# Pairs of output tiles of the gated feed-forward by seven products of quarters, in a two-layer decoder step

## The reference

```
D_MODEL = 1024;  D_FF = 2816
def rms_norm(x, g):
    xf = x.astype(jnp.float32)
    y = xf * lax.rsqrt(jnp.mean(xf * xf, axis=-1, keepdims=True) + NORM_EPS)
    return (y * g.astype(jnp.float32)).astype(x.dtype)
def swiglu(x, w_gu, w_down):
    g, u = jnp.split(x @ w_gu, 2, axis=-1)
    return (jax.nn.silu(g) * u) @ w_down
...
# in each of the two layers, behind the attention:
h = h + swiglu(rms_norm(h, g_ffn), w_gu, w_down)
```

## Time and profile before

| | |
|---|---|
| median of 3 runs | 1571.15 us (1570.95 to 1577.21) |
| the profiled execution | 1575.01 us, its span 1572.5 us |
| PE busy | 1441.2 us, 92% of the span |
| DVE / ACT / POOL busy | 427.7 / 338.4 / 197.9 us |
| moved between HBM and the chip's memory | 235.75 MB |
| granted clock of PE, mean | 0.933 of full speed |

### The profile page before, as it was taken

One profiled execution on the slowest core, in us unless ns is written; L12 is line 12 of the kernel. 1 busy time (PEld: TensorE's weight loads), 2 busy tenths in 40 slices (PEclk: granted clock), 3 DMA queues, 4 the chain that ended last, 5 costly groups with the idle time before them and its releaser, 6 DMA issues.

```text
span 1572.5 us, 22763 instructions
## 1 busy us (share of the span) xinstructions
PE 1441.2 (92%) x8680; PEld 1054.4 (67%) x8680; DVE 427.7 (27%) x1061; ACT 338.4 (22%) x885; POOL 197.9 (13%) x315
## 2 busy tenths in 40 slices
PE   7996889689899999999999999978788799999996
PEld 4454667457787788777777764675545477777775
DVE  2606454431222120111110017627534212111000
ACT  2115443321222120110000001336633201000000
POOL 0111292000000000211110111150022211111000
PEclk9995999789999999999999999857799799999998
DMA  7349687675355530334333451440056644342340
GB/s 276 108 134 359 219 312 243 232 257 174 114 170 168 195 112 0 101 114 158 109 127 111 144 181 59 148 126 1 1 161 203 214 160 161 107 160 99 110 139 30
DMA packets 145620, 235.75 MB, mean 150 GB/s; under 512 B 9554, under 2 KB 101970, under 8 KB 145106
## 3 DMA queue, kind: packets, MB, share of 16 engines
q1 hardware_dynamic: 140386, 212.39, 40.3%
q0 software_dynamic: 5136, 22.05, 4.1%
HBM read 229.09 MB, written 13.64 MB: 154 GB/s over the span
## 4 chain that ended last, share of the span: by engine, by line
PE 84%; DVE 5%; ACT 4%; DMA 3%; SPq 2%; issue 2%; POOL 0%; DVEq 0%; ACTq 0%; POOLq 0%
PE ps L653 22%; PE ps L732 14%; PE ps L672 11%; PE ps L474 10%; PE ps L438 9%; PE ps L636 4%; PE ps L573 2%; PE ps L752 2%; PE ps L618 2%; PE ps L859 1%; PE ps L479 1%; ACT big L984 1%; DMA ring<-in_state_win 1%; DMA ring<-in_cache_kv 1%; SPq L314 1%
## 5 line engine op out<-in xcount | busy, mean ns | idle before, releaser
L653 PE MATMUL ps<-qT,ring 128*128 128x288 f32 x1408 | 342.1, 406 | 0.0
L653 PEld LDWEIGHTS ps<-qT,ring 128*128 128x128 f32 x1408 | 267.9, 190 | 73.6
L732 PE MATMUL ps<-big,proj 128*128 128x252 f32 x1024 | 228.0, 380 | 0.0
L732 PEld LDWEIGHTS ps<-big,proj 128*128 128x128 f32 x1024 | 192.7, 192 | 27.0 <-issue 5.0
L984 ACT ACTIVATE big<-ps 64x256 f32<-64x256 f32 (+3 forms) x300 | 135.7, 466 | 206.3 <-PE ps L438 204.9
L672 PE MATMUL ps<-big,ring 128*128 128x288 f32 x704 | 171.3, 407 | 4.1 <-POOL big L1702 4.1
L438 PE MATMUL ps<-ct,ring 128*128 128x128 f32 x960 | 146.8, 300 | 19.9 <-DMA ring<-in_cache_kv 8.9
L672 PEld LDWEIGHTS ps<-big,ring 128*128 128x128 f32 x704 | 133.8, 190 | 41.6 <-POOL big L1702 5.0
L474 PE MATMUL ps<-ring,xT 128*128 128x512 f32 (+1 forms) x384 | 159.4, 574 | 2.5 <-DMA ring<-in_w_in 2.5
L438 PEld LDWEIGHTS ps<-ct,ring 128*128 128x128 f32 x960 | 114.8, 152 | 63.2 <-issue 37.7
L474 PEld LDWEIGHTS ps<-ring,xT 128*128 128x128 f32 x384 | 70.4, 192 | 84.0 <-issue 81.3
(11 more groups left out here) (233 smaller groups left out, 1183.1 us busy)
## 6 DMA issues: line engine op xcount, KB each, us to landing
ring<-in_cache_kv SPq DMA_DIRECT2D x128, 512.0 KB, 5.8
ring<-in_w_gu SPq DMA_DIRECT2D x44, 1024.0 KB, 7.4
ring<-in_w_in SPq DMA_DIRECT2D x11, 2048.0 KB, 7.9
ring<-in_w_down SPq DMA_DIRECT2D x16, 1408.0 KB, 5.9
ring<-in_cache_kv SPq DMA_DIRECT2D x64, 256.0 KB, 3.0
ring<-in_w_out SPq DMA_DIRECT2D x4, 2048.0 KB, 7.8
ring<-in_cache_kv SPq DMA_DIRECT2D x64, 128.0 KB, 3.0
ring<-in_state_win SPq DMA_DIRECT2D x16, 512.0 KB, 5.8
```

The source lines that it names most:

```text
L653: last = mm(ps[2 * (f % 3) + y][:, 0:T], src[:, k, y * 256 + j * P:y * 256 + (j + 1) * P], x2T[:, k, :], start=k == 0, stop=k == KD - 1)
L732: last = mm(ps[j % 2][:, 0:NKV * NCS], w1r(j // 2, o)[:, (j % 2) * P:(j % 2 + 1) * P], KC[:, b % 2, (j // 2) * 4:(j // 2) * 4 + 4, o % 8, ...
```

## The change

Gate, up and down take a pair of output tiles as one 2x2 problem: output tiles j = 0, 1; halves kh = 0, 1 of the inner dimension; halves t = 0, 1 of the 288 tokens (144 each). Before, that is 8 quarter products (as 4 products of full width). Now it is seven (Strassen's scheme in the form of Winograd), each of 144 columns, with four sums of weight quarters, four sums of activation quarters and seven additions of the results. Step n = 0 of gate/up stays as it was, since the norm's factor is not ready then; from step 1 on the moving operand is normed beforehand (`norm_x`: `xT = x2T * rst`), so the scaling of every output tile falls away. The loops of gate/up are written out, and PE waits at a product for the sum that it needs.

```
+GU_ORDER = (1, 2, 3, 5, 6, 7, 4)
+GU_SUMS = {5: 0, 6: 1, 7: 2, 3: 3}
+DOWN_ORDER = ((1, 5, 2, 6, 7, 3, 4), (1, 2, 4, 5, 6, 7, 3), (1, 2, 4, 5, 6, 7, 3), (1, 2, 5, 6, 7, 3, 4))
...
 # SP: a slot of down is taken again only when its sums are made too
+                    if before[0] == "down":
+                        sp.wait_ge(d_w, NDW * before[1] + 4 * (before[2] // 2 + 1))
...
 # PE, gate/up (line 691 after), bank group 0-2 for gate, 3-5 for up
+                for n in range(1, GU_STEPS):
+                    lhs = gu_weights(pe, l, n)
+                    for y in range(2):
+                        out = gu_out(y)
+                        if (n, y) == (1, 0):
+                            pe.wait_ge(u_u[l], 1)
+                        else:
+                            pe.wait_ge((u_g, u_u)[y][l], n + 1)
+                        for x in GU_ORDER:
+                            if y == 0 and x in GU_SUMS:
+                                pe.wait_ge(u_w, NUW * l + 4 * (n - 1) + GU_SUMS[x] + 1)
+                            if n == 1 and y == 0:
+                                pe.wait_ge(u_x, NUX * l + need_t[x])
+                            for k in range(4):
+                                last = mm(out[x], lhs[x][:, k, y, :], rhs[x][:, k, :], start=k == 0, stop=k == 3)
                         last.then_inc(u_p[l], 1)
...
 # PE, down (line 716 after)
+                for x in DOWN_ORDER[cg]:
+                    if x in DOWN_SUMS:
+                        pe.wait_ge(d_w, NDW * l + 4 * cg + DOWN_SUMS[x] + 1)
+                    for k in range(HK):
+                        last = mm(out[x], lhs[x][:, k, :], rhs[x][:, k, :], start=k == 0, stop=k == HK - 1)
                     last.then_inc(d_p[l], 1)
...
 # DVE
+                def sum_gu(n):
+
+                    w = gu_weights(dve, l, n)
+                    if n >= 3:
+                        dve.wait_ge(u_p[l], 2 * (n - 1))
+                    ops = ((5, w[0], w[4], ALU.add), (6, w[5], w[1], ALU.subtract), (7, w[1], w[0], ALU.subtract),
+                           (3, w[2], w[6], ALU.subtract))
...
+                def add_gu(n, y):
+
+                    dve.wait_ge(u_p[l], 2 * n + y + 1)
+                    if y == 0:
+                        dve.wait_ge(u_a[l], n)
+                    else:
+                        dve.wait_ge(u_e[l], n)
+                    link(v.tensor_copy(u2, m[1]))
+                    tt(c[:, 0, 0, :], u2, m[2], ALU.add)
+                    link(tt(u2, u2, m[6], ALU.add))
+                    tt(u4, u2, m[5], ALU.add)
+                    link(tt(u3, u2, m[7], ALU.add))
+                    tt(c[:, 0, 1, :], u4, m[3], ALU.add)
+                    tt(c[:, 1, 1, :], u3, m[5], ALU.add)
+                    tt(c[:, 1, 0, :], u3, m[4], ALU.add).then_inc((u_g, u_u)[y][l], 1)
...
+                for n in range(1, GU_STEPS):
+                    if n + 1 < GU_STEPS:
+                        sum_gu(n + 1)
+                    elif n + 1 == GU_STEPS:
+                        sum_act(0, 7)
+                        sum_weights(0, 0, 2)
+                    add_gu(n, 0)
+                    add_gu(n, 1)
+                    if n == 6:
+                        dve.wait_ge(u_e[l], HK // 2 + 1)
+                        tt(tsum[0], act[0][1], act[0][0], ALU.subtract).then_inc(d_x, 1)
+                sum_weights(0, 2, 4)
+                sum_act(7, HK)
+                for cg in range(4):
+                    if cg < 3:
+                        sum_weights(cg + 1)
+                    add_down(cg)
```

More of the change, by code:

```diff
@@ L272, in ffn_plan @@
             for n in range(8):
-                plan.append((("down", l, n), d_p[l], n + 1))
+                last = (1, 2)[n % 2], (1, 4)[n % 2]
+                done = max(DOWN_ORDER[n // 2].index(x) for x in last) + 1
+                plan.append((("down", l, n), d_p[l], 7 * (n // 2) + done))
         ffn_plan(0)
@@ L350, in _ @@
                 kind = name[0]
[L351 to L365, removed]
                 if kind == "late":
@@ L639, in ffn @@
             def ffn(l):
[L640 to L653, removed]
-                                          x2T[:, k, :], start=k == 0, stop=k == KD - 1)
-                        last.then_inc(u_p[l], 1)
-                        if f == 0:
-                            mean_cols(2 * l + 1)
@@ L659, in ffn @@
[L659 to L673 removed]
+                src = take(pe, "gu", l, 0).rearrange("p (k n) -> p k n", k=8)
@@ new lines, in ffn @@
+                for j in range(2):
+                    for y in range(2):
+                        for k in range(KD):
+                            if j == 0 and y == 0:
+                                pe.wait_ge(n_x[2 * l + 1], k + 1)
+                            last = mm(ps[3 * j + y][:, 0:T], src[:, k, y * 256 + j * P:y * 256 + (j + 1) * P],
+                                      x2T[:, k, :], start=k == 0, stop=k == KD - 1)
+                    last.then_inc(u_p[l], 1)
+                    if j == 0:
+                        mean_cols(2 * l + 1)
@@ L1145, in ffn @@
                 f(rst, R[:, 3, T:2 * T], ACT.Sqrt).then_inc(n_rs[2 * l + 1], 1)
[L1147 to L1158 removed]
+                for n in range(GU_STEPS):
+                    act.wait_ge(u_g[l], 2 if n == 0 else n + 2)
+                    if n:
+                        act.wait_ge(u_e[l], n)
+                    f(R[:, 1, 0:2 * T], R[:, 0, 0:2 * T], ACT.Silu).then_inc(u_a[l], 1)
             def compress(n):
@@ new lines, in ffn, with sum_act @@
+                sum_squares(2 * l + 1)
+                if l == 1:
+                    dve.wait_ge(s_kv, 48 + 16 * 5 + 16 * NB)
+                sum_gu(1)
+                norm_cols(2 * l + 1)
+                scale(0)
+                norm_x()
+                scale(1)
+                act = [[actT[:, kh * HK:(kh + 1) * HK, t * HT:(t + 1) * HT] for t in range(2)] for kh in range(2)]
+                def sum_act(lo, hi):
+                    a = [[x[:, lo:hi, :] for x in row] for row in act]
+                    t = [x[:, lo:hi, :] for x in tsum]
+                    dve.wait_ge(u_e[l], (HK + hi) // 2)
+                    tt(t[2], a[1][1], a[0][1], ALU.subtract).then_inc(d_x, 1)
+                    tt(t[1], a[1][1], t[0], ALU.subtract).then_inc(d_x, 1)
+                    dve.wait_ge(d_x, NDX * l + (3 if lo == 0 else 6))
+                    tt(t[3], a[1][0], t[1], ALU.subtract).then_inc(d_x, 1)
```

174 lines of the change are left out of this document (117 added, 57 removed).

## The result

| | before | changed |
|---|---|---|
| median (runs) | 1571.05 us (4) | 1509.64 us (4) |
| lowest to highest | 1570.34 to 1577.21 | 1505.93 to 1510.96 |
| ratio, 95% interval | 1 | 0.9597 (0.9567 to 0.9627) |

The kernel became faster by 61.4 us, with 1514 forecast and 1505 to 1540 as the range. A second series of five runs of the changed kernel gave 1510.52 us and 0.960 (0.9578 to 0.9623).

A forecast was written before the change was run, and what follows sets the result against it. PE's matmul passes were taken as the bound in the feed-forwards. Passes -55.8, POOL's wait -4.1 and new waits +3 gave -56.9 on the profiled 1575.0, so 1518.1; set against the runs' median, 1514 us, range 1505 to 1540.

The forecast's parts named there:

- Passes after: Gate/up steps 1 to 10 and down: 3472 passes of 144 columns at 0.1225 us, 425.3 us, a gain of 55.8.
- The rule that spoke against it: Skill's 81 against 56 ns for 128 columns: a pass would cost 0.177 us, the kernel would be slower by 130.
- The wait that goes: Down's start: the 2.07 us wait for POOL in each layer goes, a gain of 4.1 us, from below 0.
- New waits on PE: Gate/up and down: 170 matmuls carry a wait, if already met costing between 0 and 7.6 us; 3 taken.
- DVE: Sums and additions in gate/up and down: 9.2 us against PE's 13.7 a step, 4 in hand; cost taken as 0.
- The load in the open: Rival: every pass pays part of its weight load; a loss above 0.1386 us a pass, about 1745 at 0.190; 5%.
- DVE as the bound: Rival in gate/up: DVE's operations take 1.6 times as long, a step 14.7 us, 1540 in all; 8%.
- Passes costlier at waits or shapes (0.1275): Rival: passes cost 0.1275 us, no gain at POOL's wait: -30.8, about 1540, half of that at 1525; 17%.
- The clock: Rival: the clock is granted at 0.50 and every term doubles; 2%.

## Why the prediction held, step by step

**Passes after: right.** 0.1225 us was forecast from a straight line through 252 and 288 columns, held against a floor of 0.113; 137.20/1120 gives 0.1225, and the four stretches take 425.73 us where 425.3 was forecast. The floor is 0.1117. That the line hit so well needed a reading finer than the one written down: a row of 16 with its last record taken as 0.37 us gives 0.2133 for 252 columns, 0.81 ns a column and 0.126 us at 144, a gain of 44 and not 56. The mean record of these passes is 0.380 (the page's row of line 732), and with it the row gives the 0.2127 us and the 0.83 ns that were used. From two widths 36 columns apart, every error is four times as large at 144. The record of a load, 190 ns, is longer than the pass itself, so it could not be read as a price.

**The rule that spoke against it.** PE's passes stand 0.1225 us apart at 144 columns and 0.1117 at 128, in an unbroken stream of loads and matmuls. The Trainium skill (TensorE: Matmul & The Clock Gate, Back-to-back issue gap) has about 81 ns for 128 columns in such a stream, where its figure without the loads is about 56. The prediction's estimate by that ratio was 0.177; the measurement decides against carrying it over, with 0.1225. At 128 columns something does stand above the line here, but by 2.5 ns (0.1117 against 0.1092).

**The wait that goes: right, a little small.** 4.1 us was the idle column; by the starts it is 4.7 (2.34 a layer), and 3.3 to 8.3 by the times of the first kernel with that wait alone removed.

**New waits on PE: mis-sized.** 3 us were taken; a wait that is met costs nothing that shows. In layer 0 104 of the matmuls carry a wait, and 103 of them start 0.122 or 0.123 us after the one before, as the others do. The one left is the fourth product of down, with the 0.14 us above; that is 0.3 us in all. The 0.045 us for each wait was a misreading: in the row of 48 passes the excess stands at the first distance (0.317 us), and the pass that waits comes 0.212 us after the one before. The stretch of 672 passes has waits in it too and still gives 0.2425.

**The tail: left out.** In layer 1 PE waits 0.40 us for DVE after the last down product where it was 0.91 in the kernel before: -0.5, of which the sum had nothing. The last addition has 144 columns instead of 288, which fits, but no run takes it alone.

The sum was -55.8 - 4.1 + 3 = -56.9. By the starts it is -55.8 - 4.7 + 0.3 - 0.5 = -60.7, which is what the feed-forwards differ by. The result lies 4.4 us under the forecast, 2.7 of them the waits.

**DVE: right in what it decides, wrong in one size.** Forecast were 9.2 us a step and 4 in hand; a plain step keeps DVE for 10.0 us (730.11 to 740.14) and 3.5 are in hand. (102.1/10 = 10.2 is the busy time averaged over the ten steps, with the sums of the normed input and of act in it.) `sum_gu` was to take 4.8 us and takes 5.8, POOL's product 1.4 and takes 2.26, both because they take turns: without DVE's sums the product takes 1.41. The Trainium skill (GPSIMD Engine Reference, the table of specifications) has POOL share its memory interfaces with VectorE and contend with operations that have two SBUF inputs; the trace agrees, at 1.09 us for one sum of a step, under the bound of 1.4. Of the three places where DVE stands nearest, the normed tiles for step 1 were in time (made from 671.17 to 673.79, first asked for at 675.03). The passage to down had 1.34 in hand with 1.4 forecast, in part by luck: the act sum at 801.93 took 2.42 us beside POOL where 1.2 was counted, and a wait for the transfer and some round figures that had been counted did not come. The act sums for the fourth product had 0 in hand where 1.0 was forecast, since a sum of 1408 columns at 816.07 took 2.83 us beside POOL, and 1.62 alone. The sums for the second pair of down wait for their transfer until 825.26 (26.75 us from the start of step 10, with 26 forecast) and are needed at 41.

**The rivals.** The load in the open: refuted by 0.1225. DVE as the bound: it is not, and the two runs with doubled sums show how far off it is. At +2.3 us a step nothing happens but in one step of ten. At +4.6 DVE's plain step is 14.60 us, 0.88 above PE's 13.72; so its break-even is at about 3.7 us more a step. That rival's 1540 does not come out of its own terms: 20 us, and as much again, on 1514 is 1554. Passes costlier at waits or shapes (0.1275): not seen. The 0.1275 was no distance between equal passes: in that row the first distance is 0.166 and the change to line 573 takes 0.202, and the six between are 0.109 or 0.110. The clock: 1.00 in all four stretches. The lower end of the range, 1505, should have been 1506 by its own terms (1571.15 - 65.1).

What stays open: why the clock was granted differently to the same code in the two profiled executions, where nearly all of the 7.7 us lie, and what makes the floor of 0.1117.

## What to carry to other kernels

Before cutting a matmul into more and narrower passes, find in the trace the distance of passes at two widths, as far apart as it has them and from start to start, and the floor at a narrow one, and put the new width on that line; never take the record of a load for its price. Seven products for eight save an eighth of the columns, and of the time only as long as the halved tile stays above the floor: here 7 x 0.1225 = 0.858 against 4 x 0.2425 = 0.970, while a tile of 128 columns cut in two halves of 64 would pay 7 x 0.1117 = 0.78 where the whole tile pays 4 x 0.1117 = 0.45, a loss. Then list where the engine that makes the sums stands nearest to PE's need, with what runs beside it on POOL counted as its own time.

## What the runs showed of the hardware

- Passes of 64, 96, 112 and 128 moving columns with full 128x128 weights all take 0.1117 us at clock 1.00; 144 take 0.1225 and 288 0.2425. Transposes of 128 columns take 0.109.
- The clock stays at 1.00 at 64 columns. In the kernel before it was at 0.50 in a stretch of 60 columns, which PE entered after 2.77 us of waiting; with doubled sums it fell to 0.50 behind a wait of 2.36 us, and not behind waits of 1.19 or less. At 0.50 a pass of 144 columns takes 0.240 us. In the kernel before it did not fall behind 2.07 us at down's start.
- A semaphore wait that is already met costs PE nothing that shows: 0.122 or 0.123 us to 103 passes with one, and 0.1225 without. One that just misses costs 0.14 us.
- A sum by DVE of two operands in SBUF and a product by POOL take turns by whole operations, as far as their times tell: 2.31 against 1.22 us for DVE's sum of 1024 columns, 2.26 against 1.41 for POOL's product of 576, and 1.07 us for a POOL product of 16 columns that arrives during a sum.
- Equal code takes equal time at equal clock (84.76 and 84.77 us at 1.00), and two executions differ where the clock does (18.20 us at 0.63, 13.70 at 0.93).
